# Winograd-Strassen products for six tile pairs per up-projection, low parts of weights by adding DMAs

## The chip, the cores and the metric

The kernel runs on one core of one Trainium2 chip. The metric is the device time of one execution in microseconds. All arithmetic counts as float32: TensorE works on operands of the type fp32r, and a float32 operand is given to it as a high part and a low part.

## What is computed

A trunk of four layers for one sequence of 512 frames, with 16 learned positions ahead of it, so 528 positions of 1,024 channels. Each layer is a token mixer (latent attention, a gated linear recurrence, a state-space layer, retention) and a gated feed-forward network. Both are residual branches behind a root-mean-square norm. The change touches the feed-forward network's first product:

```python
def conv_glu_ffn(a, w_up, conv_w, conv_b, w_down):
    u = a @ w_up                                   # (528, 1024) @ (1024, 5632)
    u = lax.conv_general_dilated(u, conv_w[:, None, :], window_strides=(1,),
        padding=[(CONV_WIDTH - 1, 0)], feature_group_count=u.shape[-1], ...) + conv_b
    gate, val = jnp.split(u, 2, axis=-1)
    return (jax.nn.silu(gate) * val) @ w_down      # (528, 2816) @ (2816, 1024)

for i in range(DEPTH):
    a = rms_norm(h, norm_mix_g[i])
    h = h + mixer_i(a)
    h = h + conv_glu_ffn(rms_norm(h, norm_ffn_g[i]), ffn_w_up[i], ffn_conv_w[i], ffn_conv_b[i], ffn_w_down[i])
```

## The kernel before

Channels lie on the 128 partitions and positions along the free dimension, so the residual `h` is eight tiles of 128 x 528. The eight stages follow each other: attention, feed-forward 0, recurrence (hgrn), feed-forward 1, state space (s5), feed-forward 2, retention, feed-forward 3.

**Weights** come as a stream of 416 units of 512 KB, a unit being up to eight 128 x 128 blocks side by side. Each goes through a ring of four slots (`RING`), and its preparation is ordered three units ahead of its use (`AHEAD`). SP loads a unit into `raw` (`load_unit`, L209). ScalarE writes the high part, rounded to fp32r, into `wr[:, s, 0]` once TensorE is done with the unit of four before (`round_unit`, L220). The low part `raw - high` goes to `wr[:, s, 1]` (`split_unit`, L228). GpSimd makes it, except in the up-projections, where VectorE does. SP loads the slot's next unit when the low part is made.

**A product** (`project`, L251) of a 128 x 128 weight block with a moving operand takes three passes: high x high, high x low, low x high. Each pass runs in two halves of 264 positions (`HALF`). An output tile of the up-projection sums eight blocks: 8 x 3 x 2 = 48 matmuls. The moving operand `xs` is `h` times the norm's gain, in high and low part; the norm's root `rstd` is multiplied in afterwards.

**A feed-forward stage** has an up part of 22 pairs (`KT`), a gate tile and a value tile each, in eleven rounds of two pairs, and a down part of eight tiles with 22 blocks each, from units of 8, 7 and 7 blocks (`DOWN`). For each up tile VectorE (`turn` in `ffn_dve`) multiplies by `rstd` out of PSUM (L480), splits a weight unit (L228), and makes the three taps of the convolution (L489, L492, L495). Then come silu on ScalarE (L537), the product of gate and value (L499), its high part on ScalarE (L540) and its low part on VectorE (L471), all into `hid`. PSUM holds four tiles (`tile(g)`), and `tile_free` counts those that were read. The last feed-forward stage leaves out columns that the result doesn't need (`c0`, `project_real` L237).

Each engine has its own program; they wait for each other by semaphores that count (`unit_done`, `lo_ready`, `hi_ready`). GpSimd does nothing else in feed-forward stages than to split the down part's units.

## Time and profile before

| | us |
|---|---|
| median of three runs | 2873.75 |
| lowest, highest | 2871.77, 2875.95 |
| profiled execution, its own time | 2873.11 |
| its span (first to last instruction) | 2871.3 |
| TensorE busy | 2759.5 |
| VectorE, ScalarE, GpSimd busy | 1827.2, 943.0, 671.4 |

Busy time is the time in which an engine runs some instruction of the program. Matmuls overlap in the records, so the 284 ns that a record lasts is not what a matmul costs; that is read from how many start in a stretch. PE is TensorE, PEld its loading of weights, DVE VectorE, ACT ScalarE, POOL GpSimd, and SP issues DMAs.

### The profile page before, as it was taken

How to read it: one execution, taken by the hardware profiler on the slowest of the kernel's cores; microseconds unless marked ns; L12 is line 12 of the kernel's file. 1: busy time of each engine (PE TensorE's matmuls, PEld its weight loads, DVE VectorE, ACT ScalarE, POOL GpSimd, SP SyncE). 2: the span in 40 equal slices, each digit the busy share in tenths (PEclk: the TensorE clock that was granted, in tenths of full speed). 3: DMA queues.
4: the chain of work that ended last, by engine and by line, in shares of the span. 5: the costliest groups of instructions: out<-in, count | busy, mean ns of one | idle time of the engine just before them, and what ended most of it. 6: DMA issues, size and time to landing. Idle time of an engine off the chain costs nothing. (4 is left out here: it accounts for less than half of the span.)

```text
span 2871.3 us, 57559 instructions
## 1 busy us (share of the span) xinstructions
PE 2759.5 (96%) x23004; PEld 2667.5 (93%) x23004; DVE 1827.2 (64%) x2764; ACT 943.0 (33%) x1423; POOL 671.4 (23%) x327
## 2 busy tenths in 40 slices
PE   8999999998999999999789999999999999999999
PEld 7779999998888999999678999999999999899987
DVE  6664777415777777789795687731353545787730
ACT  5663222223444322221364222222222223322221
POOL 3112000243222300013532300024334324200033
PEclk9999999999999999999889999999999999999999
DMA  4101222332111222222201222233322222122232
GB/s 139 39 31 59 88 88 94 104 103 73 56 57 58 71 77 94 88 97 88 84 2 38 81 95 88 95 104 101 110 78 94 68 88 74 45 96 94 94 111 80
DMA packets 65700, 231.50 MB, mean 81 GB/s; under 512 B 8192, under 2 KB 8960, under 8 KB 65056
## 3 DMA queue, kind: packets, MB, share of 16 engines
q1 hardware_dynamic: 62928, 222.56, 23.4%
q10 hardware_dynamic: 2640, 7.02, 0.7%
q8 instruction: 102, 1.67, 0.2%
q14 instruction: 30, 0.25, 0.0%
HBM read 227.45 MB, written 2.10 MB: 80 GB/s over the span
## 5 line engine op out<-in xcount | busy, mean ns | idle before, releaser
L251 PE MATMUL ps<-xs,wr 128*128 128x264 f32 (+1 forms) x12864 | 1571.2, 284 | 16.8 <-POOL wr L228 9.4
L251 PEld LDWEIGHTS ps<-xs,wr 128*128 128x128 f32 x12864 | 1555.9, 189 | 23.4 <-POOL wr L228 9.4
L228 POOL TENSOR_TENSOR wr<-raw,wr 128x1024 fp32r<-128x1024 f32 x240 | 590.4, 2466 | 2023.7 <-ACT wr L220 2023.2
L251 PE MATMUL ps<-hid,wr 128*128 128x264 f32 (+1 forms) x5376 | 656.6, 284 | 9.3 <-POOL wr L228 6.0
L251 PEld LDWEIGHTS ps<-hid,wr 128*128 128x128 f32 x5376 | 652.8, 189 | 11.2 <-POOL wr L228 6.6
L220 ACT ACTIVATE wr<-raw 128x1024 fp32r<-128x1024 f32 x416 | 434.3, 1048 | 344.6 <-PE ps L251 263.6
L480 DVE TENSOR_TENSOR ub<-ps,rstd 128x528 f32<-128x528 f32 x176 | 124.4, 707 | 143.2 <-PE ps L251 142.6
L228 DVE TENSOR_TENSOR wr<-raw,wr 128x1024 fp32r<-128x1024 f32 x176 | 214.1, 1216 | 0.0
L540 ACT ACTIVATE hid<-scr 128x528 f32 x88 | 56.8, 646 | 381.6 <-DVE scr L499 381.6
L537 ACT ACTIVATE scr<-scr 128x528 f32<-128x528 f32 x88 | 56.9, 646 | 364.3 <-DVE scr L495 364.3
L492 DVE SCALAR_TENSOR_TENSOR scr<-ub,convp,scr 128x528 f32<-128x528 f32 x176 | 135.3, 769 | 24.7 <-DVE scr L489 19.8
L495 DVE SCALAR_TENSOR_TENSOR scr<-ub,convp,scr 128x528 f32<-128x528 f32 x176 | 135.3, 769 | 23.1
L519 DVE TENSOR_TENSOR h<-ps,h 128x528 f32<-128x528 f32 x24 | 17.0, 707 | 208.7 <-PE ps L251 208.4
L237 PE MATMUL ps<-hid,wr 128*128 128x512 f32 x528 | 122.2, 393 | 0.0
L237 PEld LDWEIGHTS ps<-hid,wr 128*128 128x128 f32 x528 | 99.0, 188 | 22.9
L1808 ACT ACTIVATE work<-work 128x528 f32<-128x528 f32 (+2 forms) x120 | 57.5, 517 | 159.7 <-DVE work L1667 60.4
L489 DVE TENSOR_SCALAR scr<-ub,convp 128x528 f32<-128x528 f32 x176 | 96.6, 549 | 0.1
L382 DVE SCALAR_TENSOR_TENSOR xs<-h,gains,xs 128x528 fp32r<-128x528 f32 x56 | 71.5, 1284 | 24.1 <-ACT xs L366 23.2
L366 ACT ACTIVATE xs<-h,gains 128x528 fp32r<-128x528 f32 x56 | 41.0, 736 | 131.7 <-DVE h L519 75.1
L516 DVE TENSOR_TENSOR h<-ps,h 128x512 f32<-128x512 f32 x8 | 5.5, 692 | 110.5 <-PE ps L237 110.5
L357 DVE TENSOR_TENSOR sqsum<-sqsum,scr 128x528 f32<-128x528 f32 x64 | 70.3, 1098 | 8.3 <-ACT scr L374 6.4
L374 ACT ACTIVATE scr<-h 128x528 f32<-128x528 f32 x64 | 40.4, 633 | 85.9 <-DVE h L519 82.6
(303 smaller groups left out, 2311.7 us busy)
## 6 DMA issues: line engine op xcount, KB each, us to landing
raw<-in_stream SPq DMA_DIRECT2D x416, 512.0 KB, 3.4
work<-in_ret_tab ACTq DMA_DIRECT2D x4, 1056.0 KB, 5.5
h<-in_h SPq DMA_DIRECT2D x8, 264.0 KB, 6.0
out<-h SPq DMA_DIRECT2D x8, 256.0 KB, 4.3
work<-in_s_b ACTq DMA_DIRECT2D x1, 512.0 KB, 3.7
work<-in_s_c ACTq DMA_DIRECT2D x1, 512.0 KB, 5.0
convp<-in_convp ACTq DMA_DIRECT2D x4, 88.0 KB, 2.2
work<-in_mla_tab ACTq DMA_DIRECT2D x1, 264.0 KB, 2.6
```

The lines of the kernel that those rows point to most:

```text
L220: act.activation(wr[:, s, 0].rearrange("p a b -> p (a b)"), raw[:, s, :], ACT.Copy).then_inc(hi_ready, 1)
L228: pool.tensor_tensor(wr[:, s, 1].rearrange("p a b -> p (a b)"), raw[:, s, :], wr[:, s, 0].rearrange("p a b -> p (a b)").bitcast(F32), ALU. ...
L237: mm = pe.matmul(out[:, 0:SEQ], wr[:, slot, w, k], x[k][v][:, META:T], start=start and k == 0 and p == 0, stop=stop and k == len(x) - 1 an ...
L251: mm = pe.matmul(out[:, q, c:HALF], wr[:, slot, w, b0 + k], x[k][v][:, q * HALF + c:(q + 1) * HALF], start=start and k == 0 and p == 0, st ...
L357: dve.tensor_tensor(sqsum[:], sqsum[:], scr[:, 2 + m % 2], ALU.add)\
L382: eng.scalar_tensor_tensor(xs[:, m + 4 * i, 1], h[:, m + 4 * i], gain_of(n, m, i), xs[:, m + 4 * i, 0].bitcast(F32), ALU.mult, ALU.subtrac ...
L480: dve.tensor_tensor(halves(ub[:, s, 2:]), tile(gg + q), halves(rstd[:]), ALU.mult)\
L489: dve.tensor_scalar(scr[:, s], ub[:, s, 2:], cp(2), cp(3), ALU.mult, ALU.add)\
L492: dve.scalar_tensor_tensor(scr[:, s], ub[:, s, 1:T + 1], cp(1), scr[:, s], ALU.mult, ALU.add)\
L495: dve.scalar_tensor_tensor(scr[:, s], ub[:, s, 0:T], cp(0), scr[:, s], ALU.mult, ALU.add)\
L537: act.activation(scr[:, 2], scr[:, 0], ACT.Silu).then_inc(up_act.sem, up_act.one(("silu", j)))
L1808: act.activation(out, x, func, **kw).then_inc(o.sem, o.one(name))
```

## The change

**Seven products for eight.** From round 1 to round 6 the second pair of each round is no longer two tiles of 48 matmuls. Its gate tile and value tile, the two halves of the sum over channels and the two halves of the positions make a 2 x 2 by 2 x 2 block product. It is done with seven block products of 4 blocks x 3 passes = 12 matmuls. A round (`quad`) then has six units in place of four: gate and value of the first pair as before, one unit of unchanged blocks (used by two products), and three units of mixed weights (two, two and one product). VectorE puts the results together from PSUM through `probs`.

**Mixed weights.** The sums of weight blocks are made on the chip, in a new DRAM buffer `mixed`, 18 units per layer. `mix` does it in four steps per layer with GpSimd's DMAs: a copy of 18 units (9.44 MB), then adding DMAs of 6.29 MB, 3.15 MB and 1.57 MB. For layer 0 they stand at the start of the kernel and in the attention stage. For a later layer, the copy stands in the up part of the feed-forward stage ahead of it and the adding ones in that stage's down part.

**Mixed activations.** Four sums of quarters of the normed input are needed in high and low part. ScalarE writes the full-precision input `xfull` (eight tiles), GpSimd forms the sums and their low parts, ScalarE the high parts. They use space of `hid` that is not yet written.

**Low parts of weights.** In the whole kernel, ScalarE now writes the high part twice, once negated into `wr[:, s, 1]`, and GpSimd issues a DMA that adds `raw` to it. Consumers and the next load wait for that DMA (`lo_landed`). VectorE and GpSimd split no weights any more.

```diff
+            act.activation(wr[:, s, 1].rearrange("p a b -> p (a b)"), raw[:, s, :], ACT.Copy, scale=-1.0).then_inc(hi_ready, 1)
...
-            pool.wait_ge(hi_ready, u0 + i * per + 1)
-            pool.tensor_tensor(wr[:, s, 1].rearrange("p a b -> p (a b)"), raw[:, s, :],
-                               wr[:, s, 0].rearrange("p a b -> p (a b)").bitcast(F32), ALU.subtract).then_inc(lo_ready, 1)
+            pool.wait_ge(hi_ready, 2 * (u0 + i * per + 1))
+            pool.sem_inc(low_begun, 1)
+            pool.dma_start(wr[:, s, 1].rearrange("p a b -> p (a b)"), raw[:, s, :].bitcast(F32R), accum_op=ALU.add)\
+                .then_inc(lo_landed[s], 16)
...
+        def product_pe(pe, out, slot, b0, x):
+            for k in range(len(x)):
+                for p, (w, v) in enumerate(((0, 0), (0, 1), (1, 0))):
+                    mm = pe.matmul(out, wr[:, slot, w, b0 + k], x[k][v], start=k == 0 and p == 0,
+                                   stop=k == len(x) - 1 and p == 2)
...
+            def quad(i, c):
+                u, g = ug + 4 + 6 * c, gg + 4 + 4 * c
+                r = 6 * layer + c + 2 * i
+                slot = lambda k: (u + k) % RING
+                s1, s2 = tile(g + 2), tile(g + 3)
+                low_wait(pe, u, i, 12)
+                pe.wait_ge(tile_free, g - 3 + i * 8)
+                project(pe, tile(g), slot(0), 0, x, True, True, unit_done, c0=c0)
+                low_wait(pe, u + 1, i, 12)
+                pe.wait_ge(tile_free, g + i * 8)
+                product_pe(pe, s2[:, 0], slot(1), 0, b11)
+                product_pe(pe, s1[:, 0], slot(1), 4, b21).then_inc(unit_done, 1)
+                low_wait(pe, u + 2, i, 12)
+                pe.wait_ge(t_pool.sem, t_pool.done("l1", layer))
+                product_pe(pe, s1[:, 1], slot(2), 0, t1)
+                pe.wait_ge(t_pool.sem, t_pool.done("l2", layer))
+                product_pe(pe, s2[:, 1], slot(2), 4, t2).then_inc(unit_done, 1)
+                low_wait(pe, u + 3, i, 12)
+                project(pe, tile(g + 1), slot(3), 0, x, True, True, unit_done, c0=c0)
+                low_wait(pe, u + 4, i, 12)
+                pe.wait_ge(t_pool.sem, t_pool.done("l4", layer))
+                pe.wait_ge(fast_dve.sem, fast_dve.done("e1", r))
+                product_pe(pe, s2[:, 0], slot(4), 0, t4)
+                pe.wait_ge(fast_dve.sem, fast_dve.done("c11", r))
+                product_pe(pe, s1[:, 0], slot(4), 4, b22).then_inc(unit_done, 1)
+                low_wait(pe, u + 5, i, 12)
+                pe.wait_ge(t_pool.sem, t_pool.done("l3", layer))
+                pe.wait_ge(fast_dve.sem, fast_dve.done("e16", r))
+                product_pe(pe, s2[:, 1], slot(5), 0, t3).then_inc(unit_done, 1)
...
+            def quad(r):
...
+                dve.wait_ge(unit_done, u + 2)
+                one("e1", dve.tensor_copy(part1, s2[:, 0]))
+                dve.wait_ge(o.sem, o.done("e1", f))
+                one("c11", dve.tensor_tensor(left(1), part1, s1[:, 0], ALU.add))
+                dve.wait_ge(unit_done, u + 3)
+                dve.wait_ge(o.sem, o.done("c11", f))
+                one("e16", dve.tensor_tensor(part1, part1, s2[:, 1], ALU.add))
+                dve.wait_ge(o.sem, o.done("e16", f))
+                one("d", dve.tensor_tensor(right(1), part1, s1[:, 1], ALU.subtract))
...
+                dve.wait_ge(unit_done, u + 5)
+                dve.wait_ge(o.sem, o.done("d", f))
+                one("c12", dve.tensor_tensor(right(1), right(1), s1[:, 0], ALU.add))
+                dve.wait_ge(o.sem, o.done("c12", f))
...
+                dve.wait_ge(unit_done, u + 6)
+                dve.wait_ge(o.sem, o.done("row1", f))
+                one("e167", dve.tensor_tensor(part1, part1, s2[:, 1], ALU.add))
+                dve.wait_ge(o.sem, o.done("e167", f))
+                dve.tensor_tensor(right(0), part1, s1[:, 1], ALU.subtract).then_inc(tile_free, 1)
+                dve.tensor_tensor(left(0), part1, s2[:, 0], ALU.subtract).then_inc(tile_free, 1)
+                dve.wait_ge(tile_free, g + 4)
+                one("row2", dve.scalar_tensor_tensor(ub[:, 0, 2:], ub[:, 0, 2:], -1.0, rstd[:], ALU.mult, ALU.mult))
...
+            round_unit(act, u0 + AHEAD)
+            act.wait_ge(tail_hi.sem, tail_hi.done("hi", 8 * n + DT - 1))
+            act.wait_ge(norm_dve_done.sem, norm_dve_done.done(("n", LAST), n))
+            for k in range(DT):
+                act.activation(xfull[:, k], h[:, k], ACT.Copy, scale=gain_of(n, k, 0)).then_inc(t_act.sem, t_act.one(f"x{k}"))
+            silu(0, 0)
+            round_unit(act, u0 + AHEAD + 1)
+            high_sum(1)
+            high_sum(2)
+            hi(0, 0)
+            round_unit(act, u0 + AHEAD + 2)
+            high_sum(4)
+            silu(1, 0)
+            round_unit(act, u0 + AHEAD + 3)
+            high_sum(3)
+            hi(1, 0)
+            for r in range(1, 7):
+                u = u0 + 4 + 6 * (r - 1) + AHEAD
+                round_unit(act, u)
+                if r > 1:
+                    silu(1, r - 1)
+                round_unit(act, u + 1)
+                if r > 1:
+                    hi(1, r - 1)
+                round_unit(act, u + 2)
+                silu(0, r)
+                round_unit(act, u + 3)
+                round_unit(act, u + 4)
+                round_unit(act, u + 5)
+                hi(0, r)
...
+        def mix(pool, layer, k):
+            to = mixed[6 * layer:6 * layer + 6]
+            of = lambda name: a["mix_" + name][6 * layer:6 * layer + 6]
+            done = mixed_done[layer]
+            near, far = slice(0, 4 * P), slice(4 * P, 8 * P)
+            def add(unit, cols, name):
+                pool.dma_start(to[:, unit, :, cols], of(name)[:, :, 0:cols.stop - cols.start], accum_op=ALU.add, max_dma_last_dim=4096)\
+                    .then_inc(done, 16)
+            if k == 0:
+                pool.dma_start(to, of("base"), max_dma_last_dim=4096).then_inc(done, 16)
+            elif k == 1:
+                pool.wait_ge(done, 16)
+                add(0, slice(0, 8 * P), "22")
+                add(1, far, "21")
+                add(2, near, "21")
+            elif k == 2:
+                pool.wait_ge(done, 64)
+                add(0, far, "11")
+                add(1, far, "11")
+            else:
+                pool.wait_ge(done, 96)
+                add(1, far, "12")
...
+            full = lambda k0, q: xfull[:, k0:k0 + 4, q * HALF:(q + 1) * HALF]
+            b11, b12, b21, b22 = full(0, 0), full(0, 1), full(4, 0), full(4, 1)
+            summed = lambda t: tplain[:, t - 1, :, 1]
+            split_unit(pool, u0 + AHEAD)
+            pool.wait_ge(t_act.sem, t_act.done(f"x{DT - 1}", layer))
+            total("t1", 1, b12, b11, ALU.subtract)
+            total("t2", 2, summed(1), b22, ALU.subtract)
+            split_unit(pool, u0 + AHEAD + 1)
+            rest(1)
+            total("t4", 4, summed(2), b21, ALU.add)
+            split_unit(pool, u0 + AHEAD + 2)
+            rest(2)
+            total("t3", 3, b22, b12, ALU.subtract)
+            split_unit(pool, u0 + AHEAD + 3)
+            rest(4)
+            rest(3)
+            if layer + 1 < DEPTH:
+                mix(pool, layer + 1, 0)
+            for u in range(4, UP_UNITS):
+                split_unit(pool, u0 + AHEAD + u)
...
+            for u in range(3 * DT):
+                if u in (0, 8, 16):
+                    mix(pool, layer + 1, 1 + u // 8)
+                split_unit(pool, ug + AHEAD + u)
...
+                    if u - u0 in (4, 9, 14):
+                        mix(pool, 0, (u - u0 + 1) // 5)
...
+                sp.wait_ge(mixed_done[layer], 112)
+                for u in range(4, 40):
+                    if u in MIXED:
+                        load_mixed(sp, u0 + u, skipped)
+                        skipped += 1
+                    else:
+                        load_unit(sp, u0 + u, skipped=skipped)
...
+            mix(pool, 0, 0)
...
+            for k in range(2, 14, 2):
+                out += [_unit(up[k]), _unit(up[k + 1]), _unit(up[KT + k])]
+            for k in range(14, KT):
+                out += both(k)
```

TensorE around rounds 1 to 6 of a feed-forward stage, before (a loop over rounds, each of its turns four tiles from `xs`):

```order
L435 ISA
L429 REGISTER_ALU
L251 MATMUL ps<-xs,wr 128x264 x48
L428 REGISTER_ALU
L429 REGISTER_ALU
L251 MATMUL ps<-xs,wr 128x264 x48
L429 REGISTER_ALU
L251 MATMUL ps<-xs,wr 128x264 x48
L429 REGISTER_ALU
L251 MATMUL ps<-xs,wr 128x264 x48
```

and TensorE at the same place with the change, the first quad of the loop's turn (`hid` holds the mixed activations there):

```order
L284 MATMUL ps<-xs,wr 128x264 x48
L486 REGISTER_ALU
L459 MATMUL ps<-xs,wr 128x264 x24
L459 MATMUL ps<-hid,wr 128x264 x24
L284 MATMUL ps<-xs,wr 128x264 x48
L222 ISA
L498 ISA
L459 MATMUL ps<-hid,wr 128x264 x12
L500 REGISTER_ALU
L459 MATMUL ps<-xs,wr 128x264 x12
L504 REGISTER_ALU
L459 MATMUL ps<-hid,wr 128x264 x12
```

Two groups of 48 have become 24, 24, 12, 12 and 12, taken from four units.

GpSimd from the start through the attention stage into feed-forward 0, before:

```order
L2995 UNCONDITIONAL_BRANCH
L228 ISA
L228 TENSOR_TENSOR wr<-raw,wr 128x1024 x27
L572 UNCONDITIONAL_BRANCH
L572 ISA
```

and with the change, from the first sum of activations in feed-forward 0 to the copy for layer 1 and on:

```order
L765 TENSOR_TENSOR tplain<-xfull 128x4x264
L765 TENSOR_TENSOR tplain<-tplain,xfull 128x4x264
L261 DMA wr<-raw 128x1024
L770 TENSOR_TENSOR hid<-tplain,hid 128x4x264
L765 TENSOR_TENSOR tplain<-tplain,xfull 128x4x264
L261 DMA wr<-raw 128x1024
L770 TENSOR_TENSOR hid<-tplain,hid 128x4x264
L765 TENSOR_TENSOR tplain<-xfull 128x4x264
L261 DMA wr<-raw 128x1024
L770 TENSOR_TENSOR hid<-tplain,hid 128x4x264 x2
L748 DMA mixed<-in_mix_base 2304x1024
L261 DMA wr<-raw 128x1024 x52
```

The splits have become DMAs, with eight sums of 4 x 264 columns and the copy among those of feed-forward 0. The down part of that stage, in GpSimd's program with the change:

```order
L745 DMA mixed<-in_mix 6x128x1024
L745 DMA mixed<-in_mix 6x128x512 x2
L261 DMA wr<-raw 128x1024 x8
L745 DMA mixed<-in_mix 6x128x512 x2
L261 DMA wr<-raw 128x1024 x8
L745 DMA mixed<-in_mix 6x128x512
L261 DMA wr<-raw 128x1024 x12
```

Three groups of adding DMAs stand among the weights' own, eight units apart.

## Rows read from the trace of the kernel before

**Rows 1.** Page, part 1: busy us (share of the span) xinstructions.
```profile
PE 2759.5 (96%) x23004; PEld 2667.5 (93%) x23004; DVE 1827.2 (64%) x2764; ACT 943.0 (33%) x1423; POOL 671.4 (23%) x327
```
**Rows 2.** Chain that ended last, feed-forward 2: start us, us, what.
```profile
1647.42 376.04 PE ps L251 x3120
```
**Rows 3.** Windows, feed-forward 0, up and down: us, busy us by engine, clock, DMA share.
```profile
289.00:543.50 254.50, 254.50 (x2113) 254.50 (x2113) 198.83 (x265) 71.09 (x89) 4.17 (x2) 1.00 0.28 91
543.50:672.00 128.50, 128.50 (x1071) 128.16 (x1070) 21.94 (x37) 35.09 (x40) 55.57 (x24) 1.00 0.33 107
```
**Rows 4.** Timeline, one up tile of feed-forward 0: start us, us, engine, line.
```profile
440.05 0.71 DVE L480 TENSOR_TENSOR ub<-ps,rstd 128x528 f32<-128x528 f32 x1 [1.03 <-PE ps L251]
...
441.81 0.55 DVE L489 TENSOR_SCALAR scr<-ub,convp 128x528 f32<-128x528 f32 x1
...
442.51 0.77 DVE L492 SCALAR_TENSOR_TENSOR scr<-ub,convp,scr 128x528 f32<-128x528 f32 x1 [0.15 <-DVE scr L489]
...
445.07 0.65 ACT L540 ACTIVATE hid<-scr 128x528 f32 x1 [4.42 <-DVE scr L499]
```
**Rows 5.** Timeline of GpSimd, one unit of the down part.
```profile
603.27 2.40 POOL L228 TENSOR_TENSOR wr<-raw,wr 128x1024 fp32r<-128x1024 f32 x1 [1.55 <-ACT wr L220]
```
**Rows 6.** Lines 228 and 220: duration ns min/median/max, first and last start us.
```profile
L228 POOL TENSOR_TENSOR wr<-raw,wr x240: 2347/2397/2949, 7.0 to 2849.3; 128x1024 fp32r<-128x1024 f32 x120
L228 DVE TENSOR_TENSOR wr<-raw,wr x176: 1211/1217/1221, 293.8 to 2751.1; 128x1024 fp32r<-128x1024 f32 x176
...
L220 ACT ACTIVATE wr<-raw x416: 1038/1045/1063, 5.9 to 2848.2; 128x1024 fp32r<-128x1024 f32 x139
```
**Rows 7.** DMA view: packets, MB, share; then KB each, us to landing; SP's issues.
```profile
q1 hardware_dynamic: 62928, 222.56, 23.4%
...
raw<-in_stream SPq DMA_DIRECT2D x416, 512.0 KB, 3.4
...
gains<-in_gains SPq DMA_DIRECT2D x1, 32.0 KB, 1.9
pick<-in_pick SPq DMA_DIRECT2D x1, 2.0 KB, 6.8
...
8.12 0.45 SPq L2923 DMA_DIRECT2D pick<-in_pick  x1
```
**Rows 8.** Timeline, start of feed-forward 0.
```profile
276.34 5.95 PE L251 MATMUL ps<-xs,wr 128*128 128x264 f32 x48
...
277.29 0.74 ACT L366 ACTIVATE xs<-h,gains 128x528 fp32r<-128x528 f32 x1 [3.57 <-DVE h L400]
...
286.22 0.30 DVE L306 SCALAR_TENSOR_TENSOR rstd<-ub 128x132 f32<-128x132 f32 x1
...
289.31 42.92 PE L251 MATMUL ps<-xs,wr 128*128 128x264 f32 x354
```
**Rows 9.** Timelines of GpSimd and TensorE, first part of the attention stage.
```profile
9.95 5.72 POOL L228 TENSOR_TENSOR wr<-raw,wr 128x1024 fp32r<-128x1024 f32 x2 [0.56 <-ACT wr L220]
...
37.11 9.52 POOL L228 TENSOR_TENSOR wr<-raw,wr 128x1024 fp32r<-128x1024 f32 x4 [7.74 <-ACT wr L220]
51.71 2.40 POOL L228 TENSOR_TENSOR wr<-raw,wr 128x1024 fp32r<-128x1024 f32 x1 [5.08 <-ACT wr L220]
...
9.45 5.74 PE L251 MATMUL ps<-xs,wr 128*128 128x264 f32 x24 [9.45 <-POOL wr L228]
...
34.81 6.06 PE L251 MATMUL ps<-xs,wr 128*128 128x264 f32 x48 [0.89 <-DVE rstd L340]
...
64.59 1.61 PE L251 MATMUL ps<-halfs,wr 128*128 128x264 f32 x12
```
**Rows 10.** Window of 97 to 101 us; timeline of TensorE in two heads of attention.
```profile
97.00:101.00 4.00, 4.00 (x23) 4.00 (x22) 3.40 (x3) 3.29 (x7) 2.90 (x2) 0.57 0.43 131
...
96.53 2.33 PE L251 MATMUL ps<-halfs,wr 128*128 128x264 f32 x12 [2.35 <-DVE keyed L1104]
...
117.11 1.74 PE L251 MATMUL ps<-halfs,wr 128*128 128x264 f32 x12 [1.42 <-DVE keyed L1104]
```

More of the change, by code:

```diff
@@ L54 @@
 DOWN = (8, 7, 7)
+ROUNDS = KT // 2
+UP_UNITS = 2 * KT + 12
+MIXED = tuple(4 + 6 * q + k for q in range(6) for k in (2, 4, 5))
 RH, RDK, RDV = 4, 256, 512
@@ L174, in trunk @@
         hi_ready = sem("hi_ready")
-        lo_ready = sem("lo_ready")
+        lo_landed = [sem(f"lo_landed{s}") for s in range(RING)]
+        low_begun = sem("low_begun")
         unit_done = sem("unit_done")
@@ L434, in ffn_pe @@
                 up(s, 0)
-            with pe.Fori(1, KT // 2) as i:
+            with pe.Fori(0, 3) as i:
+                for c in range(2):
+                    quad(i, c)
+            with pe.Fori(0, ROUNDS - 7) as i:
                 for s in range(4):
-                    up(s, i)
-            ug, gg = u0 + 2 * KT, gg + 2 * KT
+                    up(s, i, 28, 12)
+            ug, gg = u0 + UP_UNITS, gg + 2 * KT
             end = (layer + 1) * (KT // 2) - 1
@@ L543, in ffn_act @@
+            silu(1, 6)
+            hi(1, 6)
+            with act.Fori(7, KT // 2) as i:
+                for s in range(4):
+                    round_unit(act, u0 + 12 + AHEAD + s, i, 4)
+                    (hi if s % 2 else silu)(s // 2, i)
+            ug = u0 + UP_UNITS
             setup = setup_of(n + 1)
```

207 lines of the change are left out of this document (138 added, 69 removed).

## The prediction

> **What bounds the kernel now.** I read the busy times first: TensorE is at work for 96% of the span and nothing else is above 64% [rows 1]. The chain that ended last is then mostly one row repeated: 3,120 matmuls of line 251 in 376.04 us in the third feed-forward stage [rows 2]. That is 0.1205 us for a matmul with 264 columns, in an unbroken run. The stage table agrees: in the up-projection and in the down-projection TensorE is busy for the whole of the window at clock 1.00, the 2.4 GHz level, while DMA is busy for 28 to 33% [rows 3]. So a matmul taken out of an up-projection is worth 0.1205 us, as long as the weights come in time. The question of this change is the second half of that sentence.
>
> How much time there is for the weights follows from the ring of four slots. A slot is free when its matmuls are over, and its next unit is wanted three units later. A full up unit is 48 x 0.1205 = 5.78 us, so 17.3 us; a down unit is 128.5 / 24 = 5.35 us, so 16.1 us [rows 3]. Of this the kernel uses in the down stage only ScalarE's 1.05 and GpSimd's 2.40 us [rows 5, 6]. In the up stage VectorE makes the low part in 1.22 us between its other steps [rows 6].
>
> **What it takes away.** Each of the six quads of a layer replaces two tiles of 48 matmuls by seven products of 12. The saving is 96 - 84 = 12 matmuls, over four layers 24 x 12 x 0.1205 = **-34.7 us**. The last layer's gain is a little smaller, since its tiles already leave out columns; I let that go. VectorE loses 176 splits of 1.217 us and GpSimd 240 of 2.397 us [rows 6]. Neither is on the chain, so I count nothing for it; it could be worth some us where VectorE leads in the mixers.
>
> **Weights' low parts, ordinary stretches.** ScalarE now writes a unit twice, 2 x 1.045 us [rows 6]. Then comes a DMA of 512 KB that adds. No row shows an adding DMA. A plain 512 KB load lands in 3.4 us; the main queue moved 222.56 MB in 23.4% of the span, which is 331 GB/s when it moves, so 512 KB take 1.58 us of the 3.4 [rows 7]. An addition must also read its destination, so it costs between once and twice that movement: 3.4 to 5.0 us. I take the middle, 4.2, and the same factor of 1.5 on all adding DMAs. Ready after 2.1 + 4.2 = 6.3 us (plus issue) against 16.1 to 17.3: hidden. Only the kernel's first unit has no cover; TensorE waited for it until 9.45 us, and its low part now takes 1 to 3 us more, its second write 1 [rows 9]: **+3 us**.
>
> **Inside a quad** the units last 5.78, 2.89, 2.89, 5.78, 2.89 and 1.45 us, 21.7 in all. The least that three of them in a row make is 1.45 + 2.89 + 5.78 = 10.1 us, still above 6.3. ScalarE's load is 12 x 1.05 + 4 x 0.65 = 15.1 us, VectorE's four sets of taps (2.1 each), four full-width steps around them (0.71 each), two products, two low parts and eight half-width steps (about 0.4) make some 17 us, both under 21.7 [rows 4]. The DMA engines must move 1.58 us of load and 1.5 x 1.58 = 2.37 us of add per unit, 23.7 us a quad against 21.7, if loads and adds never overlap. They are two queues, so I cost the steady state at nothing and put 24 x 2 = 48 us on the upper end.
>
> **Start of each feed-forward stage.** Before the first quad GpSimd makes four sums and four low parts of 1,056 columns. By its split of 1,024 columns (2.397 us) that is 8 x 2.5 = 20 us, with the weights' DMAs of units 4 to 7 queued in between. It can begin when ScalarE has made eight full-width copies after the norm's root: the root is there at 286.5 us in the first stage, eight times 0.74 us more give 292.4 [rows 8]. GpSimd's row from there is two sums, unit 4's DMA, a low part and a sum, unit 5's, a low part and a sum, unit 6's, two low parts, unit 7's; at 2.5 us a step and 1 for issuing a DMA (an estimate from the 0.4 to 0.5 us of SP's rows, doubled) it has issued unit 6's at about 310 and unit 7's at about 317 [rows 7, 8]. TensorE starts the first tile at 276.34, the third at 289.31 [rows 8] and wants unit 4 at 300.9, unit 5 at 306.7, unit 6 at 309.6 and unit 7 at 312.5. With 4 us per landing I get waits of 1, 1, 3 and 4 us, **9 us per stage, +36 us**. If the GpSimd sums go faster or overlap better it is 6, if they collide with VectorE 11. This alone gives the saving back.
>
> **The mixing DMAs** build the sums of weights in DRAM, on the queue that now also carries every unit's low part. Per layer: a copy of 9.44 MB, then adds of 6.29, 3.15 and 1.57 MB. At 331 GB/s the copy takes 28.5 us, the adds 19.0, 9.5 and 4.8, or 1.5 times that: 28.5, 14.2, 7.1. Does a small transfer wait behind them? The start of the kernel shows it: 2 KB of `pick` took 6.8 us to land behind the loads of `h` on the same queue, while 32 KB of `gains`, first in it, took 1.9 [rows 7]. The Trainium skill ("DMA: Bandwidth & Descriptors", section on queues, rings and completion order) says that an engine takes the descriptors of one ring in order; by that rule the low parts of all units behind a mixing step wait it out, and the trace agrees.
>
> The copy is issued after the GpSimd sums and ahead of unit 7, which is already late there. All of it shows: 28.5 us. In the down stage a step delays its next unit by (its time + 2.1 + 4.2 - 16.1): 28.5 - 9.8 = 18.7, 14.2 - 9.8 = 4.4, and nothing for the third. Sum 51.6 us, in three stages **155 us**. The first layer's steps stand in the attention stage. The copy starts at about 16 us and ends at 44.2; unit 3's low part lands after that, wanted at 34.81 [rows 9]: 13 us. The first add is issued after unit 7's low part, some 5 us before unit 8's (46.6 and 51.71 us before), and unit 8 is wanted at 64.59 [rows 9]: issued near 58 on the delayed clock it ends near 86.5 with unit 8 at 90.7 against 77.6: 13 us. The other two find units of 19 us each. Together **+26 us**.
>
> **Clock.** After TensorE had worked in pieces, the granted clock was 0.57 from 97 to 101 us, and 12 matmuls took 2.33 instead of 1.74 us and the 36 behind them longer too [rows 10]: some 1.7 us for each such place. With ten waits of 4 to 30 us: **+17 us**, from 0 to 40.
>
> **Sum**: -34.7 + 3 + 36 + 155 + 26 + 17 = +202. On the profiled execution's 2873.1 us that makes 3075; the median of the runs, 2873.75, is the same within its spread. With adds at plain speed, 6 us at the starts and no clock loss: -34.7 + 3 + 24 + 3 x (28.5 + 9.2) + 16.5 = +122, 2995. With adds at half speed, 11 us at the starts and 40 for the clock: -34.7 + 3 + 44 + 3 x (28.5 + 28.2 + 9.2) + 35 + 40 + 48 = +333, 3206.
>
> **Rivals.**
> 1. *The mixing hides.* If the engines serve the small DMAs in turn with the large ones, or move DRAM to DRAM much faster than 331 GB/s, the 155 + 26 + 17 us go. For it: DMA is idle 70% of the time [rows 3], and there are 370 us for each layer's 30 MB. Against it: the row of `pick`. It gives 2873 - 34.7 + 3 + 36 = 2878; if GpSimd's sums also fit ahead of the first quad, 2845. This is the way to a faster kernel. Chances 0.08 and 0.16.
> 2. *The adds are narrow.* The adds go to blocks of the form 6 x 128 x 1024. If their six blocks were shared out over six of 16 engines instead of all, the first takes 524 KB an engine at 20.7 GB/s, x 1.5 = 38 us, the next two 19 each. Stage: 28.5 + 28.2 + 9.2 + 9.2 = 75 us, attention 36: 3155. The Trainium skill (same page, section on why a DMA increments its semaphore by 16) has the rule that the slowest dimension sets the number of engines, here six; no row tells. Chance 0.18.
> 3. *The DMA engines become the bound.* If an add costs two movements, a unit of a quad needs 1.58 + 3.16 = 4.74 us of all engines against 3.62 of TensorE. Six units lack 6.7 us, 24 quads 161; with the mixing at that price, 3 x (51.6 + 14.3) + 35 for the 181, it is 2873 - 35 + 3 + 36 + 17 + 161 + 233 = 3288. It decides from 1.3 movements per add on, if nothing overlaps. Against it: a ring of four lets a quad borrow from the full units beside it. Chance 0.08.
> 4. *No gain from the products* (their matmuls alternate operands and might run slower than 0.1205): adds up to 35 us to any case; inside their ranges.
>
> **Chances.** Forecast (small DMAs held back, 2995 to 3206, likeliest 3075) 0.50, rivals as above. Faster by over 0.2% (what a measurement of this kernel can tell from no change) is the second half of rival 1, 0.16; within 0.2% most of the other half, 0.05; slower 0.79. The range from 2850 to 3250 leaves out rival 3 and the lower part of rival 1.
>
> **What would show it.** Right: the chain shows TensorE waiting for `wr` 10 to 40 us at a time, once early in the first three feed-forward stages and once or twice in their down stages, ended by a DMA; the last stage shows only its start. In the quads, groups of 12 and 24 matmuls at 0.12 us with no gaps. The adding DMAs of `wr` land in 4 to 5 us alone and in over 20 behind a mixing step. The wait before unit 4 to 7 in every stage, the last too, shows the price of GpSimd's sums. Wrong: if these DMAs land in under 10 us while a mixing step is moving, rival 1 holds; if they land in over 8 us everywhere, rival 3.

## The result and the profile after

The changed kernel takes **3596.01 us** (median of 4 runs, 3589.53 to 3602.97), beside 2872.76 us for the kernel before. The ratio is 1.2512 [1.2497, 1.2527]: 723 us slower, where 202 were forecast, and 346 us above the upper end of the range. The profiled execution takes 3589.53 us with a span of 3587.6, at a mean clock of 0.891.

Parts 1, 3, 5 and 6 of the page of the changed kernel answer to [rows 1, 7]:

```profile
PE 2794.4 (78%) x22716; PEld 2694.1 (75%) x22716; DVE 1628.6 (45%) x2780; ACT 1469.9 (41%) x1983; POOL 621.5 (17%) x611
...
q0 software_dynamic: 125632, 325.34, 47.2%
q1 hardware_dynamic: 69840, 247.73, 20.3%
...
L284 PE MATMUL ps<-hid,wr 128*128 128x264 f32 (+1 forms) x5376 | 675.1, 289 | 417.9 <-DMA wr<-raw 413.9
...
L745 POOL DMA_DIRECT2D mixed<-in_mix x24 | 47.7, 1990 | 378.4 <-issue 378.2
...
wr<-raw POOLq DMA_DIRECT2D x464, 512.0 KB, 6.3
...
mixed<-in_mix_base POOLq DMA_DIRECT2D x4, 9216.0 KB, 33.3
...
mixed<-in_mix POOLq DMA_DIRECT2D x20, 1536.0 KB, 24.5
mixed<-in_mix POOLq DMA_DIRECT2D x4, 3072.0 KB, 46.6
```

TensorE has 288 matmuls fewer, and its share of the span fell from 96% to 78%. The new queue q0 carries the adding DMAs and the four plain copies. Its packets take 47.2% of the 16 DMA engines' span, 325.34 MB in 1,693 us or 192 GB/s, where SP's queue moved 331 [rows 7]. A low part lands in 6.3 us. The adds of the mixing land in 46.6 us for 3 MB and 24.5 us for 1.5 MB, and GpSimd itself stands still for 378 us ("issue") ahead of them.

Where TensorE waits is seen in the timelines of the first feed-forward stage. Its start, GpSimd and TensorE (start us, us, engine, line, and in brackets the idle time before and what ended it):

```profile
403.21 2.96 POOL L765 TENSOR_TENSOR tplain<-xfull 128x1056 f32<-128x1056 f32 x1 [8.39 <-ACT xfull L682]
...
414.61 6.07 PE L284 MATMUL ps<-xs,wr 128*128 128x264 f32 x48 [2.09 <-DVE ub L575]
424.47 4.71 PE L459 MATMUL ps<-xs,wr 128*128 128x264 f32 x24 [3.79 <-DVE ub L575]
...
431.52 4.60 PE L459 MATMUL ps<-hid,wr 128*128 128x264 f32 x24 [2.35 <-DMA wr<-raw]
433.46 1.16 POOL L748 DMA_DIRECT2D mixed<-in_mix_base  x1 [0.30 <-POOL hid L770]
434.60 2.68 POOL L261 DMA_DIRECT2D wr<-raw  x3
468.89 7.57 PE L284 MATMUL ps<-xs,wr 128*128 128x264 f32 x48 [32.76 <-DMA wr<-raw]
```

TensorE's last row follows the copy of line 748. The timeline of the same two engines in the down part:

```profile
699.19 1.95 POOL L745 DMA_DIRECT2D mixed<-in_mix  x1 [0.61 <-issue]
747.36 1.95 POOL L745 DMA_DIRECT2D mixed<-in_mix  x1 [46.22 <-issue]
771.97 1.91 POOL L745 DMA_DIRECT2D mixed<-in_mix  x1 [22.66 <-issue]
773.03 4.47 POOL L261 DMA_DIRECT2D wr<-raw  x4
...
798.78 31.49 PE L284 MATMUL ps<-hid,wr 128*128 128x264 f32 x242 [86.17 <-DMA wr<-raw]
```

The three adds of the first step go out 48 and 25 us apart, each about when the one before has landed; the low parts behind them aren't issued until 773. TensorE stands for 86.2 us. The second and third step cost 37.3 and 13.6 us in the same stage. These waits, 32.8 + 86.2 + 37.3 + 13.6, come to 170 us in the one stage. The three stages that mix are 172, 170 and 171 us longer than in the run without mixing below, 513 in all. The attention stage, where the first layer's weights are mixed, has one wait of 20.8 us behind the copy and one of 79.2 behind the first three adds. GpSimd's timeline there:

```profile
72.22 2.20 POOL L745 DMA_DIRECT2D mixed<-in_mix  x1
118.62 1.94 POOL L745 DMA_DIRECT2D mixed<-in_mix  x1 [44.20 <-issue]
143.16 1.92 POOL L745 DMA_DIRECT2D mixed<-in_mix  x1 [22.60 <-issue]
```

While the first of these adds moves, and while the second does, little else is under way. The windows (columns as in [rows 3], the DMA engines' share last but one) show how many of the 16 engines such an add keeps busy. Six of 16 would be 0.375:

```profile
90.00:118.00 28.00, 0.82 (x4) 0.33 (x2) 2.53 (x5) 3.74 (x5) 0.00 (x0) 0.56 0.39 79
120.00:142.00 22.00, 0.00 (x0) 0.00 (x0) 0.00 (x0) 0.00 (x0) 0.56 (x1) 0.50 0.42 71
```

The last feed-forward stage has no mixing. Its windows show what the quads alone do:

```profile
3220.00:3330.00 110.00, 95.88 (x724) 93.91 (x725) 73.34 (x116) 62.90 (x71) 27.77 (x28) 0.92 0.96 232
3330.00:3380.00 50.00, 46.91 (x385) 46.20 (x385) 37.63 (x62) 28.36 (x33) 9.54 (x11) 1.00 1.02 258
3380.00:3464.00 84.00, 84.00 (x703) 83.69 (x702) 50.83 (x75) 38.79 (x46) 13.41 (x16) 1.00 0.81 186
```

The first two are the quads: TensorE is busy for 87% and 94% of them, and the DMA engines all the time (0.96, 1.02; a share can come out a little over 1). The third is ordinary tiles: TensorE is full, DMA at 0.81.

### The profile page after: what moved, and what is told of

It is laid out like the page before. It is cut to its first block and busy times, and to the rows that moved or that the text cites. A ratio compares the mean times of both kernels' runs of the same rounds, so it can differ in the third digit from the quotient of the medians.

```text
span 3587.6 us, 56527 instructions
## 1 busy us (share of the span) xinstructions
PE 2794.4 (78%) x22716; PEld 2694.1 (75%) x22716; DVE 1628.6 (45%) x2780; ACT 1469.9 (41%) x1983; POOL 621.5 (17%) x611
## 3 DMA queue, kind: packets, MB, share of 16 engines
q0 software_dynamic: 125632, 325.34, 47.2%
## 5 line engine op out<-in xcount | busy, mean ns | idle before, releaser
L284 PE MATMUL ps<-xs,wr 128*128 128x264 f32 (+1 forms) x10560 | 1329.7, 287 | 196.4 <-DMA wr<-raw 185.0
L284 PEld LDWEIGHTS ps<-xs,wr 128*128 128x128 f32 x10560 | 1305.8, 192 | 210.7 <-DMA wr<-raw 150.7
L284 PEld LDWEIGHTS ps<-hid,wr 128*128 128x128 f32 x5376 | 669.6, 193 | 421.8 <-issue 261.1
L251 ACT ACTIVATE wr<-raw 128x1024 fp32r<-128x1024 f32 x464 | 488.1, 1052 | 932.6 <-PE ps L284 482.4
L261 POOL DMA_DIRECT2D wr<-raw x464 | 408.2, 950 | 2394.2 <-ACT wr L252 2377.9
L252 ACT ACTIVATE wr<-raw 128x1024 fp32r<-128x1024 f32 x464 | 483.8, 1043 | 0.0
L459 PE MATMUL ps<-hid,wr 128*128 128x264 f32 x1152 | 157.3, 290 | 8.7 <-DMA wr<-raw 8.7
L459 PEld LDWEIGHTS ps<-hid,wr 128*128 128x128 f32 x1152 | 149.7, 194 | 10.0 <-DMA wr<-raw 9.9
L459 PE MATMUL ps<-xs,wr 128*128 128x264 f32 x864 | 120.6, 296 | 13.1 <-DVE ub L575 12.2
L459 PEld LDWEIGHTS ps<-xs,wr 128*128 128x128 f32 x864 | 115.2, 200 | 14.3 <-DVE ub L575 13.1
L671 ACT ACTIVATE hid<-scr 128x528 fp32r<-128x528 f32 (+1 forms) x88 | 56.2, 639 | 156.4 <-DVE scr L566 156.1
L270 PEld LDWEIGHTS ps<-hid,wr 128*128 128x128 f32 x528 | 99.0, 188 | 22.9
L609 DVE TENSOR_TENSOR ub<-ps,rstd 128x528 f32<-128x528 f32 x24 | 17.0, 708 | 217.4 <-PE ps L284 217.4
L745 POOL DMA_DIRECT2D mixed<-in_mix x24 | 47.7, 1990 | 378.4 <-issue 378.2
## 6 DMA issues: line engine op xcount, KB each, us to landing
mixed<-in_mix_base POOLq DMA_DIRECT2D x4, 9216.0 KB, 33.3
mixed<-in_mix POOLq DMA_DIRECT2D x20, 1536.0 KB, 24.5
mixed<-in_mix POOLq DMA_DIRECT2D x4, 3072.0 KB, 46.6
```

The costliest lines, as they stand in the source:

```text
L251: act.activation(wr[:, s, 0].rearrange("p a b -> p (a b)"), raw[:, s, :], ACT.Copy).then_inc(hi_ready, 1)
L252: act.activation(wr[:, s, 1].rearrange("p a b -> p (a b)"), raw[:, s, :], ACT.Copy, scale=-1.0).then_inc(hi_ready, 1)
L261: pool.dma_start(wr[:, s, 1].rearrange("p a b -> p (a b)"), raw[:, s, :].bitcast(F32R), accum_op=ALU.add)\
L270: mm = pe.matmul(out[:, 0:SEQ], wr[:, slot, w, k], x[k][v][:, META:T], start=start and k == 0 and p == 0, stop=stop and k == len(x) - 1 an ...
L284: mm = pe.matmul(out[:, q, c:HALF], wr[:, slot, w, b0 + k], x[k][v][:, q * HALF + c:(q + 1) * HALF], start=start and k == 0 and p == 0, st ...
L459: mm = pe.matmul(out, wr[:, slot, w, b0 + k], x[k][v], start=k == 0 and p == 0, stop=k == len(x) - 1 and p == 2)
```

## Experiments

The theory after this reading: the mixing costs about 610 us, because its adds are narrow and one waits for the other, and because all small DMAs stand behind them (rival 2 with a blocked GpSimd). The rest, some 110 us, is the quads' own: DMA engines at their limit (rival 3) and GpSimd's sums at the start. The first three runs divide the 723 us among mixing, low parts and quads.

**No mixing.** `mixed` isn't built; the quads load the base from the input.

```diff
         def mix(pool, layer, k):
+            return
...
-                sp.wait_ge(mixed_done[layer], 112)
```

> The changed kernel without its mixing DMAs: the three mixed units of each quad are loaded from the unmixed input instead (so their products are of unmixed blocks), everything else as in the change. Theory A (the low parts' adding DMAs stand behind the mixing DMAs in GpSimd's queue): the trace after the change has waits of 34, 86, 37 and 13 us in each of three feed-forward stages and of 21 and 79 us in attention, together 610 us; without the mixing they go, 3596 - 610 = 2985, between 2965 and 3005. Theory B (the DMA engines are full with the low parts' own adds, and the mixing only moves the waiting about): less than 300 us go, above 3300.

Measured: 2983.40 us, ratio 1.0377 [1.0360, 1.0394]. The mixing costs 613 of the 723 us. The three feed-forward stages that mix fall from 580, 576 and 581 us to 408, 407 and 409, and attention from 362 to 267. (A stage is counted here and below from the last matmul on `pick` in its norm to that of the next, in the profiled execution.)

**Wide adds.** The same bytes, with the partitions as the slowest dimension instead of the six blocks.

```diff
-                pool.dma_start(to[:, unit, :, cols], of(name)[:, :, 0:cols.stop - cols.start], ...
+                pool.dma_start(to[:, unit, :, cols].rearrange("q p n -> p q n"),
+                               of(name)[:, :, 0:cols.stop - cols.start].rearrange("q p n -> p q n"), ...
```

> The changed kernel with one edit: the mixing adds have the 128 partitions as leading dimension instead of the six quads. Theory A1 (an add runs on as many engines as its leading dimension allows, 6 of 16): its 3 MB land in about 19 us instead of 46.6 and its 1.5 MB in 10 instead of 24.5, the waits of 86, 37 and 13 us shrink to about 30, 10 and 0, the one of 79 in attention to 20, together about 3596 - 3 x 96 - 59 = 3250. Theory A2 (adding to DRAM is slow whatever the shape): 3596, within 30.

Measured: 3243.01 us (3238.35 to 3247.66). The page's landing of the adds, and GpSimd's timeline at the first step:

```profile
mixed<-in_mix POOLq DMA_DIRECT2D x4, 3072.0 KB, 22.9
...
643.34 4.29 POOL L745 DMA_DIRECT2D mixed<-in_mix  x3 [0.54 <-issue]
648.36 0.92 POOL L261 DMA_DIRECT2D wr<-raw  x1 [0.73 <-ACT wr L252]
```

3 MB land in 22.9 instead of 46.6 us, and GpSimd issues all three adds of the step and the low part behind them at once. Narrowness, with the blocked issue that comes with it, is worth 353 us. It is not more work for the engines: q0's packets take 51.7% of 3236.4 us here, 1,673 us, against 1,693 before the edit. The narrow adds spread the same time over fewer engines. The waits in the first stage are now 28.6 us, 10.3 and none. By the prediction's formula (step minus 9.8) these are steps of 38.4 and 20.1 us, so 6.29 MB at 164 and 3.15 MB at 157 GB/s: the "adds at half speed" of its upper case, which gave 3206.

**Low parts by adding DMA, nothing else.** The kernel before, with ScalarE's second pass and the adding DMA in place of the splits.

```diff
+            act.activation(wr[:, s, 1].rearrange("p a b -> p (a b)"), raw[:, s, :], ACT.Copy, scale=-1.0).then_inc(hi_ready, 1)
...
-            pool.tensor_tensor(wr[:, s, 1].rearrange("p a b -> p (a b)"), raw[:, s, :], ...
+            pool.dma_start(wr[:, s, 1].rearrange("p a b -> p (a b)"), raw[:, s, :].bitcast(F32R), accum_op=ALU.add)\
+                .then_inc(lo_landed[s], 16)
```

> The kernel before with one part of the change alone: all weights' low parts by a second ScalarE pass and an adding DMA; no products of the new kind, no mixing. Theory A (a landing in about 5 to 6 us is hidden behind three units of 5.3 to 5.8 us, only the kernel's start shows): 2873 + 3 to + 15, about 2880. Theory C (the adding DMAs fill the engines also in ordinary up and down parts, as the DMA share of 0.8 in the last stage's suggests): more than 2900.

Measured: 2874.55 us, ratio 1.0003 [0.9994, 1.0013]. The equal time is a balance and not a hidden cost alone. Up to the first feed-forward stage the run loses 16 us: the first unit is ready at 17.42 instead of 9.45 us, and TensorE waits 3.05 and 2.36 us more for low parts in the attention stage.

```profile
17.42 13.78 PE L258 MATMUL ps<-xs,wr 128*128 128x264 f32 x96 [17.42 <-DMA wr<-raw]
```

The recurrence (342.2 us instead of 349.5) and the feed-forward stage behind it (379.1 instead of 385.5) give 14 back. The other stages are within 1.3 us each. That VectorE's and GpSimd's freed time is what shortens these two stages is likely, but no run separates it.

In ordinary tiles the adding DMA is hidden, at a price in cover: the windows of the up and of the down part of the first feed-forward stage have TensorE full and the DMA engines at 0.81 and 0.88, where it was 0.28 and 0.33 [rows 3].

```profile
290.00:543.00 253.00, 252.68 (x2100) 252.13 (x2099) 150.43 (x227) 110.59 (x132) 37.07 (x43) 1.00 0.81 178
543.00:672.00 129.00, 129.00 (x1072) 129.00 (x1072) 22.22 (x32) 59.18 (x67) 21.52 (x25) 1.00 0.88 202
```

This gives the price of a unit. q0 moved 218.13 MB in 42.8% of 2872.7 us, 177 GB/s, so a low part of 512 KB takes 2.96 us of all engines and its load 1.6, together 4.6. Of a down unit of 5.35 us that is 86%, of an up unit of 5.78 us 79%, as the windows show. Six units of a quad need 27.5 us of the engines and TensorE gives them 21.7.

The three together say: low parts +1, quads +109, mixing +613.

**The copy on another queue.** ScalarE issues the 9.44 MB copy, with a semaphore of its own.

```diff
+            eng.dma_start(mixed[6 * layer:6 * layer + 6], a["mix_base"][6 * layer:6 * layer + 6]).then_inc(base_done[layer], 16)
...
-                pool.dma_start(to, of("base"), max_dma_last_dim=4096).then_inc(done, 16)
+                return
```

> The changed kernel with the four large copies issued by ScalarE on its own queue, at the same places. Theory A (queue order): the waits of 34 us at the first quad and of 21 in attention go nearly whole, about 25 and 15 us each, 3596 - 3 x 25 - 15 = 3505. Theory B (bandwidth: the copy keeps the engines busy for 33 us whichever queue it is on): less than 10 us per copy is gained, above 3560.

Measured: 3586.08 us (3578 to 3594), 10 us less than with the copy on GpSimd's queue, which is no more than the two runs differ by. The wait of 33 us has become two, of 17.14 and 10.86 us, both still ended by a low part. So the place in the queue alone is not what costs. One row of the page's DMA part speaks against a quick verdict, though. Queue q10 has 640 packets more than before for 37.7 MB, so 59 KB each, against packets of about 4 KB or less on the others:

```profile
q10 hardware_dynamic: 3280, 44.77, 3.5%
```

**The same in packets of 4 KB** (`max_dma_last_dim=4096` on that DMA).

> As the run with the copies on ScalarE's queue (3586), but the copy is cut into rows of 4 KB like every other DMA here; in that run it went in 640 packets of about 59 KB. Theory P (the engines serve the queues by turns, a packet each, so that long packets on one queue hold up short ones on another as much as standing behind them would): with equal packets a low part waits for one other packet per packet of its own and lands in about 8 us, the waits of 28 us at the first quads shrink to under 8 and the one in attention from 22 to under 8: 3586 - 3 x 20 - 16 = 3510, at most 3530. Theory B (the copy uses up the engines' bandwidth whichever way): 3586 within 15.

Measured: 3554.34 us (3552.81 to 3555.86), between the two expectations. Where TensorE waited 17.1 and 10.9 us it now waits 4.2 and 5.8, and then 2.3, 0.2, 1.7 and 2.0 at the units that follow. From its timeline:

```profile
431.31 5.32 PE L460 MATMUL ps<-hid,wr 128*128 128x264 f32 x24 [4.18 <-DMA wr<-raw]
442.43 7.81 PE L285 MATMUL ps<-xs,wr 128*128 128x264 f32 x48 [5.80 <-DMA wr<-raw]
...
456.92 7.43 PE L285 MATMUL ps<-xs,wr 128*128 128x264 f32 x48 [2.27 <-DMA wr<-raw]
```

The copy now takes 68.8 us to land instead of 33.3, so the engines do share. Large packets had held the small DMAs up about as long as the queue did. The Trainium skill ("DMA: Bandwidth & Descriptors", "Queues, rings and completion order") says that a DMA engine changes between queues only at the ends of packets; by that rule small packets let small DMAs through, and the two traces agree. Sharing gave back 42 us of the some 119 that the four copies had cost (3 x 32.8 + 20.8). That asks whether the rest is order or sheer engine time.

**Mixing in pieces.** 54 DMAs a layer, each 128 partitions wide and of 0.25 or 0.5 MB, issued one or two at a time behind the low parts of single units, and in the attention stage four at a time. Before it issues any, GpSimd waits until the pieces before have landed.

```diff
                 split_unit(pool, u0 + AHEAD + u)
+                if layer + 1 < DEPTH and u % 2:
+                    mix_some(pool, layer + 1, 1)
...
                 split_unit(pool, ug + AHEAD + u)
+                mix_some(pool, layer + 1, 2)
```

> The changed kernel with the mixing of each layer cut into 54 DMAs of 0.25 to 0.5 MB, 128 partitions wide, one after every second unit of the up part, two after each unit of the down part and four after each unit of attention, on GpSimd's queue as before. Nothing long stands ahead of a low part any more. Theory A (only standing in the queue costs): the mixing hides, 2983 as without it, at most 3010. Theory B (queue order matters for the narrow adds, but the rest of the price is the engines' time): copy 28.5 us and adds of 11 MB at 182 GB/s 60 us make 88 us a stage, against about 42 us that the engines were idle in feed-forward 0 of the run without mixing (0.97, 0.88 and 0.86 busy): 46 us too much in three stages, attention hides its share: 2983 + 138 = 3121, between 3070 and 3170. The run with wide adds took 3243.

Measured: 3157.32 us, ratio 1.0981 [1.0963, 1.0999]. In the first feed-forward stage (345 to 801 us) the longest wait for `wr` is now 3.3 us; there are 30 of them, 46.7 us in all. The DMA engines have no room left in its quads (0.99 from 369 to 536 us), in its ordinary up tiles or in the larger part of its down part. The windows of the latter two:

```profile
536.00:629.00 93.00, 92.73 (x767) 92.57 (x768) 58.27 (x87) 40.52 (x49) 20.22 (x24) 1.00 1.02 239
651.00:751.00 100.00, 77.34 (x573) 74.63 (x573) 8.38 (x12) 31.18 (x34) 33.27 (x39) 0.95 1.02 209
```

In the ordinary tiles TensorE is still full; in the down part it has work for 77% of the time.

Engine time comes to the right size for the 174 us above the run without mixing. A layer's mixing holds all engines for about 33 us (copy) and 11.0 MB / 0.18 = 61 us (adds), 94 in all; by the shares of q0 (53.8% of 3156.4 us against 44.8% of 2981.0 without mixing) it is 91. Free beside the kernel's own DMAs are 12% of the 129 us of the down part and about 19% of some 120 us of ordinary up tiles, 38 us. What is left over, some 55 us, is near the 48, 42 and 48 by which the three stages are longer (456, 448, 457 against 408, 407, 409). The attention stage is 40 us longer.

Order isn't cleared of all of it. In the down part of the first stage GpSimd stands for 68.7 us, 5 or so at a time, until the last two pieces have landed, and that unit's low part is issued only after the next two. As the engines are full at the same time, this run doesn't tell the two apart.

**Quads without GpSimd's sums** (and without mixing), the second operands being quarters of `xs` as they are:

```diff
-            t1, t2, t3, t4 = ([(tsum[:, t, k, 0], tsum[:, t, k, 1]) for k in range(4)] for t in range(4))
+            t1, t2, t3, t4 = part(0, 1), part(4, 1), part(0, 1), part(4, 0)
```

> The changed kernel without mixing DMAs (2983) and also without the mixed activations: no full-precision copies on ScalarE, no sums on GpSimd and their low and high parts; the products take the plain quarters of the input instead. Theory S (the sums make each feed-forward stage start late): the gaps of 2.1, 3.8, 2.7 and 1.9 us around the first quad and most of the slow clock that follows go, 4 x (10.5 + 5) = 62: 2921, between 2905 and 2935. Theory D (the DMA engines are full in the quads, and the first quad meets that as all do): less than 25 us, above 2958.

Measured: 2933.22 us (2923 to 2941), ratio 1.0215 [1.0198, 1.0232]: the sums cost 50 us, 12.5 per stage. In the first feed-forward stage TensorE still waits 14.2 us, all for `wr`.

Part of the sums' price goes by way of VectorE. In the changed kernel GpSimd is at a low part (417.62 to 420.39) and a sum (420.46 to 423.22) while VectorE makes two taps of the convolution:

```profile
417.25 3.71 DVE L556 SCALAR_TENSOR_TENSOR scr<-ub,convp,scr 128x528 f32<-128x528 f32 x1
421.00 2.80 DVE L559 SCALAR_TENSOR_TENSOR scr<-ub,convp,scr 128x528 f32<-128x528 f32 x1
```

These instructions have a median of 0.77 us. TensorE's wait of 3.8 us for `ub` ends behind them. Without the sums none of the 352 of these two lines lasts over 0.773 us, and TensorE no longer waits for `ub` in the first stage.

**Low parts over half the columns** (sums kept, no mixing):

```diff
-            pool.dma_start(wr[:, s, 1].rearrange("p a b -> p (a b)"), raw[:, s, :].bitcast(F32R), accum_op=ALU.add)\
+            pool.dma_start(wr[:, s, 1].rearrange("p a b -> p (a b)")[:, 0:4 * P], raw[:, s, 0:4 * P].bitcast(F32R), accum_op=ALU.add)\
```

> The changed kernel without mixing DMAs (2983), with each low part's DMA adding only the first half of the unit's columns (the other half keeps the negated high part). A unit then needs 1.58 us of load and 1.44 of add of all engines instead of 1.58 and 2.88, against 3.62 of TensorE in a quad. Theory D (the quads are bound by the DMA engines, busy for 0.97 there): the gaps of quads 2 to 6 and the slow clock go, 4 x (9 to 13): 2940, between 2930 and 2948; the start's gaps stay. Theory S (only the start costs): above 2970.

Measured: 2905.53 us, ratio 1.0115 [1.0098, 1.0132]: 78 us less than with whole ones, nearly twice what I expected. I had put the engines' limit at 35 to 53 us. Of the 80 us between the two profiled executions, 71 lie in the four feed-forward stages. The edit shortens two things at once: the engines' time, and the landings, those of the low parts from 6.1 to 3.8 us and those of the loads from 5.0 to 3.6.

**Both of these edits:** what seven products are worth when neither sums nor DMA engines hold them.

> Both edits together: no mixing, no mixed activations, half adds. What is left is the products themselves. If start and DMA engines are all that the products cost, this shows the saving of 12 matmuls per quad whole: 2874.5 (the kernel with low parts by DMA alone) - 34.7 = 2840, between 2836 and 2848. If the products have a price of their own (VectorE's extra steps, waits between products), it stays above 2855.

Measured: 2853.32 us, ratio 0.9933 [0.9916, 0.9950], between the two expectations. The window from 300 to 420 us, in the first quads, without the sums:

```profile
300.00:420.00 120.00, 109.40 (x866) 107.99 (x865) 77.87 (x130) 64.64 (x73) 23.52 (x27) 0.97 0.93 227
```

The same window with half adds and the sums kept:

```profile
300.00:420.00 120.00, 108.24 (x859) 107.20 (x858) 93.02 (x124) 72.92 (x84) 45.14 (x36) 0.97 0.70 169
```

The same window with both edits:

```profile
300.00:420.00 120.00, 118.97 (x976) 118.14 (x975) 87.14 (x143) 74.18 (x84) 26.80 (x31) 1.00 0.80 194
```

Each edit alone leaves TensorE 11 to 12 us of idle time and a clock of 0.97, and only both fill it. The two costs add up: 50 + 78 = 128 us against 130 for both. The run is 21 us below that with low parts alone (2874.55). By stages the two differ by 6.5, 3.0, 4.1 and 2.3 us in the feed-forward stages, **16 us** in all, and this is the products' saving. The other 5 or so lie in stages without such products, the start and attention above all, where half adds are a gain of their own.

## Why the prediction was wrong

The direction held, and so did the mechanism of the mixing's waits. The sizes did not, and the quads' own cost, put at nothing, was real.

| term | forecast, us | measured, us | from |
|---|---|---|---|
| fewer matmuls | -34.7 | -16 | both edits against low parts alone, feed-forward stages |
| low parts by DMA, ordinary stretches | +3 | +1 (16 lost, 15 gained) | low parts alone |
| GpSimd's sums, four starts | +36 | +50 | no sums against no mixing |
| whole adds in quads (DMA engines) | 0 (48 at most) | +75 | rest of the 110 without mixing |
| mixing, three stages | +155 | +513 | stages with and without mixing |
| mixing, attention | +26 | +100 | two waits; stage 95 us longer |
| clock | +17 | in the rows above | |
| sum | +202 | +723 | |

- **The adds' time is the step that failed.** The first step of a layer was put at 28.5 us, from 6.29 MB at 331 GB/s times 1.5. It took 46.6 + 24.5 + 24.5 = 95.6. Two causes multiply: 28.5 x 1.8/1.5 x 16/6 = 91, which leaves 4.6 us, 1.5 per add. An adding DMA takes 1.8 times a plain movement, not 1.5 (q0 at 177 and 182 GB/s where it has low parts alone). Its six blocks went to few engines; rival 2 had this, with 38 us for the first add where 46.6 were measured. 524 KB per engine in 46.6 us is 11.3 GB/s, and a sixteenth of 177 is 11.1, which fits six engines of 16; so does the engines' share of 0.39 and 0.42 while such adds moved. The Trainium skill ("DMA: Bandwidth & Descriptors", "Why a DMA increments its semaphore by 16 and not by 1") has the rule on the slowest dimension that rival 2 named. These traces agree with it, and it stood at 0.18 only because no row of before could bear on it. And rival 2 let a step's adds run side by side ("the next two 19 each" were other steps); in the trace one waited for the one before, through GpSimd's blocked issue, which no one of the rivals had. Whether they would have run side by side with the issue free isn't shown.
- **The formula was right.** A step delays its next unit by its time less 9.8 us: 95.6 gives 85.8 against 86.2 measured, 2 x 24.5 gives 39.2 against 37.3, 24.5 gives 14.7 against 13.6. With right durations the three stages come to 3 x (33 + 86 + 39 + 15) = 519 against 513. Rival 2's mechanism, with 1.8 for 1.5 and the adds in a row, would have given some 3470 by its own sum (an estimate: first step 91 us, the others 46 and 23, so 159 for a stage and some 95 for attention).
- **The copy**: 28.5 us forecast, a landing of 33.3 and a wait of 33 measured. Its reason, the place in the queue, was only part of it: with another queue and small packets 42 us in all came back. That the rest is engine time fits the engines' share of 1.01 while the copy moved in the changed kernel (438 to 466 us) and of 1.04 in the run with small packets (436 to 500 us); no run separates it.
- **Attention**: the first step was taken at 28.5 us, with a wait of 13; three narrow adds in a row gave a wait of 79.2 us. The copy's wait was 20.8, forecast 13.
- **The quads' steady state** was the second failed step. The working had 23.7 us of DMA against 21.7 of TensorE and dropped it, "if loads and adds never overlap". Their times add up on the same 16 engines; the windows at 0.96 and 1.02 show these full. With 27.5 us per quad the lack is 5.8 us, over 24 quads 139. Some 75 were measured; that four slots borrow the rest from the ordinary tiles around is argued, not shown. Rival 3 had that mechanism, with its price doubled (161) and a chance of 0.08, which was too low. A second reading stands untested: the way of one slot from load to low part. Without mixing it is, by the median landings, 5.0 to 5.9 us for the load, 2.1 for ScalarE, 0.9 for the issue and 6.1 for the add, 14 to 15 us, against 14.5 us that TensorE takes for four units of a quad on average (21.7 x 4/6). The working compared 6.3 us with 10.1 and left out the load. Half adds cut this way too, to some 10.5 us. As landings get longer when engines are full, the two readings aren't independent.
- **Starts**: 9 us per stage were forecast, 12.5 measured. GpSimd's sums took 2.8 us instead of 2.5. The two waits of 2.1 and 3.8 us for VectorE's `ub` (line 575) come of VectorE's long steps beside GpSimd's sums. The prediction had that only at its upper end ("if they collide with VectorE 11").
- **Clock**: in the run without mixing it was 0.94 over 120 us in the first quads, 7 us per stage. The measured rows of the table hold it already. The 17 us for all of the kernel were put at the long waits of 4 to 30 us; the loss in the quads' many short ones wasn't thought of.
- **The low parts** came out as predicted in the sum (+1 for +3), and that was luck. The start and attention lost 16 us where 3 were forecast: the first unit came 8 us later, not 3. The recurrence and the feed-forward stage behind it gave 14 back, where nothing was counted for VectorE's and GpSimd's freed time. What held is that the low parts are hidden in up and down parts.
- **The saving**: 16 of 34.7 us, against 8.7 forecast per stage. A part is the last stage's smaller tiles, which I let go. In the first stage of the run with both edits the quads themselves answer for it: they start at 334.71, 356.98, 379.18, 401.42 and 423.36 us and end at 445.17, so they last 21.8 to 22.3 us instead of 21.7, some 2.4 us for six. That is rival 4 in small. Why the second and third stage fall further short wasn't settled.
- **A slip of the working** without weight: rival 1's second figure, 2845, is 2873 - 34.7 + 3 = 2841 by its own terms.

Not shown: why GpSimd's issue waits for a narrow add to land. The wide add of the same size didn't do it, so it isn't the size. The narrow form does make more packets: q0 has 125,632 in the changed kernel and 94,912 with wide adds for the same bytes, 1,280 more per add, and no run tells whether that is the cause. Not tried: mixing in the mixer stages, where DMA has more room, and half of the low parts back on GpSimd. No complete version came below the kernel before. What one could gain in this form is some 16 us, and it has some 90 us of DMA engines per layer to hide for the mixing.

## What to carry to other kernels

Price an added DMA stream in time of all 16 engines, sum it with what they already do in that stretch, and compare with the shortest stretch of TensorE that it must feed: 27.5 against 21.7 us was the warning for the quads here, and dropping it because loads and adds are "two queues" was the error. An adding DMA counts about 1.8 plain ones, its slowest dimension should be the 128 partitions, and nothing that is wanted soon should be issued behind it. A run that keeps the saving and leaves out its costs shows early how much of it there is: 16 us of 34.7 here. And a change that leaves the time as it was should be read stage by stage: here 16 us lost and 15 gained looked like nothing.

## What the runs showed of the hardware

- Low parts by adding DMA: 177 GB/s over 16 engines (182 in the run without mixing), against 321 and 331 for the plain loads of the runs with low parts alone and before. Wide adds from DRAM to DRAM: 157 to 164 GB/s by the formula. A 9.44 MB copy from DRAM to DRAM: 33.3 us, 283 GB/s.
- The same 3 MB add: 46.6 us as 6 x 128 x 1024, 22.9 us as 128 x 6 x 1024. While narrow adds moved, the engines' share was 0.39 and 0.42.
- After a narrow add GpSimd's next DMA of the same kind was issued 48 us (3 MB) or 25 us (1.5 MB) later; after a wide one at once.
- A large DMA on another queue in packets of 59 KB delayed small ones by 28 us, and in packets of 4 KB by 10 us at the first quad, while itself taking 68.8 instead of 33.3 us.
- VectorE's steps of 0.77 us lasted up to 3.7 us while GpSimd made sums of 128 x 1056, and never over 0.773 in the run without the sums.
- Low parts by adding DMA raised the DMA engines' share in the first up part from 0.28 to 0.81 with no change in the kernel's time (1.0003). The cover was used up without a sign in the time, and the next edit paid for it.
